# Hybrid encoder layer with hierarchical experts: first gather straight from the slot table, block table between weight splits, token places on GpSimd

## The reference, cut to what matters

```python
# 4 groups x 8 experts, top-1 group, top-2 experts in it: 2048 assignments
n_blocks = -(-n_assign // 128) + 32            # slots in blocks of 128 rows
padded = ((counts + 127) // 128) * 128         # each expert starts a new block
dest = pad_start[e_sorted] + (arange(n_assign) - start[e_sorted])
slot_tok[dest] = tok_sorted;  slot_w[dest] = w_sorted
block_expert = searchsorted(pad_end, block_start, side='right')
x_blocks = h[slot_tok].reshape(n_blocks, 128, 1024)
# each block with its expert's weights, (1024 x 512), (1024 x 512), (512 x 1024):
hid = silu(xb @ w_gate[e]) * (xb @ w_up[e]);  y = hid @ w_down[e]
out = zeros.at[slot_tok].add(y * slot_w)       # and x + out, final RMSNorm
```

## Time and profile before

| | us |
|---|---|
| median of 3 runs (lowest, highest) | 1426.55 (1425.6, 1429.34) |
| the profiled execution | 1429.69 |
| its span, first to last instruction | 1428.0 |
| TensorE busy | 1321.2 (93%) |
| VectorE busy | 1093.4 (77%) |
| ScalarE busy | 861.3 (60%) |
| GpSimd busy | 413.8 (29%) |
| mean granted TensorE clock | 0.973 |

### The profile page before, as it was taken

How to read it: one execution, slowest core, us unless ns; L and a number is a source line. 1 busy time by engine, 2 the same in 40 slices (tenths; PEclk the granted TensorE clock), 3 DMA queues, 4 the chain that set the end, 5 groups by cost and what they waited for, 6 DMA issues and landing times. The chain is left out here.

```text
span 1428.0 us, 25159 instructions
## 1 busy us (share of the span) xinstructions
PE 1321.2 (93%) x8518; PEld 1115.0 (78%) x8518; DVE 1093.4 (77%) x1510; ACT 861.3 (60%) x1162; POOL 413.8 (29%) x473
## 2 busy tenths in 40 slices
PE   4999999978898879999998899999999999999984
PEld 4999778867887878668887788888888888888851
DVE  5895697775778758545667888888888888888837
ACT  7473345565566464552214777777777777777722
POOL 6020089008666737312101111111111111111140
PEclk9999999988999989999998999999999999999997
DMA  9174988412234139811016999999999999999773
GB/s 269 48 227 146 271 249 238 113 41 51 47 94 128 26 118 337 317 43 78 31 45 232 363 404 418 407 415 409 409 414 409 411 410 414 407 410 412 317 280 157
DMA packets 154825, 357.51 MB, mean 250 GB/s; under 512 B 43999, under 2 KB 100603, under 8 KB 127483
## 3 DMA queue, kind: packets, MB, share of 16 engines
q1 hardware_dynamic: 131899, 297.04, 55.8%
q0 software_dynamic: 14976, 40.43, 8.3%
q10 hardware_dynamic: 7872, 19.01, 3.4%
HBM read 287.64 MB, written 68.78 MB: 250 GB/s over the span
## 5 line engine op out<-in xcount | busy, mean ns | idle before, releaser
L2908 PE MATMUL gate_up_mm<-w_hi,gathered_T_hi 128*128 128x512 f32 x528 | 212.3, 402 | 7.7 <-DVE gathered_T_lo L3103 7.7
L2910 PE MATMUL gate_up_mm<-w_hi,gathered_T_lo 128*128 128x512 f32 x528 | 208.0, 394 | 0.0
L2909 PE MATMUL gate_up_mm<-w_lo,gathered_T_hi 128*128 128x512 f32 x528 | 207.7, 393 | 0.0
L3098 DVE TENSOR_TENSOR w_lo<-w_down,w_hi 128x2048 fp32r<-128x2048 f32 x66 | 148.5, 2289 | 54.0 <-ACT w_hi L3019 54.0
L2842 POOL COPY gather_idx<-upto_pair 128x1 int32 (+1 forms) x34 | 13.1, 385 | 510.8 <-PE x_turned L2898 470.9
L3098 DVE TENSOR_TENSOR w_lo<-first_w_gate,w_hi 128x2048 fp32r<-128x2048 f32 x66 | 150.7, 2289 | 9.5 <-ACT w_hi L3019 8.0
L3019 ACT ACTIVATE w_hi<-w_up 128x2048 fp32r<-128x2048 f32 x66 | 126.6, 1919 | 50.6 <-PE down_mm L2945 50.1
L3098 DVE TENSOR_TENSOR w_lo<-w_up,w_hi 128x2048 fp32r<-128x2048 f32 x66 | 150.6, 2287 | 4.0
L3019 ACT ACTIVATE w_hi<-w_down 128x2048 fp32r<-128x2048 f32 x66 | 125.0, 1918 | 41.2 <-issue 20.8
L3019 ACT ACTIVATE w_hi<-first_w_gate 128x2048 fp32r<-128x2048 f32 x66 | 127.0, 1925 | 32.4 <-PE gate_up_mm L2910 31.6
L2908 PEld LDWEIGHTS gate_up_mm<-w_hi,gathered_T_hi 128*128 128x128 f32 x528 | 100.4, 190 | 34.0 <-issue 12.8
(11 more groups left out here) (522 smaller groups left out, 3100.9 us busy)
## 6 DMA issues: line engine op xcount, KB each, us to landing
w_up<-in_expert_w_up SPq DMA_DIRECT2D x66, 1024.0 KB, 8.5
w_down<-in_expert_w_down SPq DMA_DIRECT2D x66, 1024.0 KB
first_w_gate<-in_expert_w_gate SPq DMA_DIRECT2D x64, 1024.0 KB, 7.6
expert_rows_dram<-ones SPq DMA_DIRECT2D x32, 512.0 KB, 6.8
expert_rows_dram<-expert_out ACTq DMA_DIRECT2D x32, 512.0 KB, 8.5
x<-s_rows_dram SPq DMA_DIRECT2D x9, 1184.0 KB, 6.9
s_rows<-s_rows_dram SPq DMA_DIRECT2D x7, 1184.0 KB, 7.5
w_raw<-in_w_in SPq DMA_DIRECT2D x12, 512.0 KB, 5.2
```

What stands on the lines that cost most here:

```text
L2908: pe.matmul(dst, xT_hi[:, k, :], hi[:, at, cols], start=k == 0, stop=False)
L2909: pe.matmul(dst, xT_hi[:, k, :], lo[:, at, cols], start=False, stop=False)
L2910: mm = pe.matmul(dst, xT_lo[:, k, :], hi[:, at, cols], start=False, stop=k == KT - 1)
L3098: dve.tensor_tensor(lo[:, at, :], flat(j), hi[:, at, :].bitcast(F32), ALU.subtract).then_inc(S["piece_lo"], 1)
```

## The change

- GpSimd's first gather takes its index straight from column 0 of the slot table, with no copy and no wait.
- `block_table` is cut in pieces, `table_starts`, `table_ends` and `table_blocks`. On TensorE the small matmuls of the second half stand behind the turning of block 0's rows; on VectorE the first split of block 0 stands ahead of `table_ends`.
- `rows_rest(0)` stands ahead of the splits 1 to 3 of block 0, `rows_out(1)` and `rows_rest(1)` stand one split earlier.
- `places` leaves VectorE. The gates stay there (`gates`, five operations). The rest is done by GpSimd in its loop, behind its two gathers: `found_places` in i = 1, `final_places` in i = 2, `turned_places` (the picks) in i = 3. The wide comparison becomes 16 operations with a scalar from a column, the reduction over 32 experts five additions by halves, and what was one operation with two steps of which one is a tensor becomes two.
- ScalarE's two exponentials stand behind the four splits of block 0.
- `keep_clock` counts are 5, 10, 16 and a new 16 behind the turning of block 1, where 12, 8 and 8 stood.

```diff
 # GpSimd
-            gather(0, 0, 1)
+            step = Steps(pool, S["small"])
+            def found_places():
+                pool.wait_ge(S["starts"], 1)
+                step(pool.tensor_scalar(E, kept["down_e"][:], -1.0, float(NEXP), ALU.mult, ALU.add))
+                step(pool.tensor_scalar(INV, kept["level"][:], 1.0, None, ALU.min))
+                step.done()
+                for n in range(2 * TT):
+                    step(pool.tensor_scalar(one_e[:, n], iota[:, 0:NEXP], small_cols[:, 0, n:n + 1], None, ALU.is_equal))
+                step.done()
+                step(TTo(one_e[:], one_e[:], starts[:, 0].rearrange("p (o e) -> p o e", o=1).broadcast_to(wide), ALU.mult))
+                step.done()
+                n = NEXP // 2
+                while n > 1:
+                    step(TTo(one_e[:, :, 0:n], one_e[:, :, 0:n], one_e[:, :, n:2 * n], ALU.add))
+                    step.done()
+                    n //= 2
+                step(TTo(small_cols[:, 1], one_e[:, :, 0], one_e[:, :, 1], ALU.add))
+            def final_places():
+                step.done()
+                step(TTo(OV, OV, kept["level"][:], ALU.add))
+                step(pool.tensor_scalar(base[:, 1:2], reach[:, TABLE - 1:TABLE], float(P), float(P), ALU.mult, ALU.subtract))
+                step.done()
...
+                step(pool.tensor_scalar(dest_f[:], place[:], -1.0, base[:, 1:2], ALU.min, ALU.add))
+                step.done()
+                pool.wait_ge(S["gate"], 5)
+                step(TTo(gate_f[:], gate_f[:], rt["gate"][:], ALU.mult))
+                step(pool.tensor_copy(dest[:], dest_f[:]))
+                step.done()
+                pool.sem_inc(S["placed"], 1)
+            def turned_places():
+                for t in range(TT):
+                    for k in range(2):
+                        pool.tensor_scalar(picks[:, t, k, :], iota[:], place[:, k, t:t + 1], rt["gate"][:, k, t:t + 1],
+                                           ALU.is_equal, ALU.mult).then_inc(S["picks"], 1)
+            pool.indirect_dma_start(out=xg[:, 0, :], out_offset=None, in_=h_dram,
+                                    in_offset=bass.IndirectOffsetOnAxis(ap=rt["slot_tok"][:, 0:1], axis=0)
+                                    ).then_inc(gathered[0], 16)
             pool.wait_ge(S["tables"], 3)
...
-                        gather(1 - s, column, b + 2)
+                        gather(1 - s, column, b + 1)
+                with pool.If(i == 1):
+                    found_places()
+                with pool.If(i == 2):
+                    final_places()
+                with pool.If(i == 3):
+                    turned_places()
 # TensorE
-            keep_clock(12)
-            block_table()
-            keep_clock(8)
+            keep_clock(5)
+            table_starts()
+            keep_clock(10)
             pe.wait_ge(gathered[0], 16)
             turn_rows(0)
-            keep_clock(8)
+            table_blocks()
+            keep_clock(16)
             pe.wait_ge(S["xT_lo"], 1)
...
             turn_rows(1)
+            keep_clock(16)
             pe.wait_ge(S["tables"], 3)
 # ScalarE
-            act.activation(kept["group"][:], kept["group"][:], ACT.Exp).then_inc(S["gates"], 1)
-            act.wait_ge(S["small"], 1)
-            act.activation(kept["top"][:, 1], kept["top"][:, 1], ACT.Exp).then_inc(S["gates"], 1)
             for j in range(2):
                 split(0, j, 16, None)
             rows_out(0)
             for j in (2, 3):
                 split(0, j, 16, None)
+            act.activation(kept["group"][:], kept["group"][:], ACT.Exp).then_inc(S["gates"], 1)
+            act.wait_ge(S["top"], 1)
+            act.activation(kept["top"][:, 1], kept["top"][:, 1], ACT.Exp).then_inc(S["gates"], 1)
             silu(2)
...
             split(1, 0, 32, 3)
+            rows_out(1)
             split(1, 1, 32, 4)
-            rows_out(1)
 # VectorE
-            block_table()
-            for j in range(2):
+            table_starts()
+            rest(0, 0, 1)
+            table_ends()
+            table_blocks()
+            rows_rest(0)
+            for j in range(1, 4):
                 rest(0, j, j + 1)
-            rows_rest(0)
-            for j in (2, 3):
-                rest(0, j, j + 1)
-            places()
+            gates()
...
             rest(1, 0, 7)
+            rows_rest(1)
             rest(1, 1, 8)
             hidden(0, 4)
-            rows_rest(1)
```

More of the change, by code:

```diff
@@ L2733, in experts @@
              "y_out idx turn small picks picked_mm picked last sum par add sq ms rt rs res "
-             "reach reach_turned past tables block_step gates placed").split()
+             "reach reach_turned past tables block_step gates top starts gate placed").split()
     S = {n: core.sem("ex_" + n) for n in names}
@@ L2847, in gather, with of @@
                                         ).then_inc(gathered[s], 16)
-            gather(0, 0, 1)
+            step = Steps(pool, S["small"])
+            TTo = pool.tensor_tensor
+            def of(n):
+                return small_cols[:, n].rearrange("p (k t) -> p k t", k=2)
+            E, OV, INV = (of(n) for n in range(3))
+            wide = [P, 2 * TT, NEXP]
+            def found_places():
[14 more added lines that the diff above has]
+                step(TTo(small_cols[:, 1], one_e[:, :, 0], one_e[:, :, 1], ALU.add))
@@ new lines, in final_places @@
+            def final_places():
[3 more added lines that the diff above has]
+                step.done()
+                step(pool.tensor_scalar(OV, OV, 1.0, None, ALU.subtract))
+                step.done()
+                step(TTo(OV, OV, E, ALU.subtract))
+                step.done()
+                step(TTo(OV, OV, INV, ALU.mult))
+                step.done()
+                step(TTo(OV, OV, E, ALU.add))
+                step.done()
+                step(pool.tensor_scalar(OV, OV, float(P), None, ALU.mult))
+                step.done()
+                step(TTo(dest_f[:], OV, kept["slot"][:], ALU.add))
+                step.done()
+                step(pool.tensor_scalar(place[:], dest_f[:], base[:, 1:2], None, ALU.subtract))
+                step.done()
+                step(pool.tensor_scalar(gate_f[:], place[:], 0.0, None, ALU.is_lt))
+                step(pool.tensor_scalar(dest_f[:], place[:], -1.0, base[:, 1:2], ALU.min, ALU.add))
+                step.done()
+                pool.wait_ge(S["gate"], 5)
+                step(TTo(gate_f[:], gate_f[:], rt["gate"][:], ALU.mult))
+                step(pool.tensor_copy(dest[:], dest_f[:]))
+                step.done()
+                pool.sem_inc(S["placed"], 1)
@@ L2850, in _ @@
+            pool.sem_inc(S["turn"], 1)
             pool.wait_ge(S["tables"], 3)
@@ L2881, in keep_clock, with table_starts @@
                     pe.matmul(y_ps[:, 0, 0:P], c["ident"][:], c["ident"][:], start=True, stop=True)
-            def block_table():
+            def table_starts():
                 pe.wait_ge(S["reach"], 2)
@@ L2888, in block_table, with table_blocks @@
                 pe.transpose(r_ps[0:NEXP, 2 * P:3 * P], starts[:, 1], c["ident"][:]).then_inc(S["reach_turned"], 1)
+            def table_blocks():
                 pe.wait_ge(S["past"], 3)
@@ L3092, in _ @@
         def _(dve):
-            small = Steps(dve, S["small"])
+            gate_step = Steps(dve, S["gate"])
             def rest(s, j, n):
@@ L3110, in hidden, with table_starts @@
                 dve.tensor_tensor(hid[:], sg[:], u_ps, ALU.mult).then_inc(S["hid"], 1)
-            def block_table():
-                step = Steps(dve, S["block_step"])
+            step = Steps(dve, S["block_step"])
+            def table_starts():
                 TTo = dve.tensor_tensor
@@ L3119, in last @@
                     return x.rearrange("p (e o) -> p e o", o=1).broadcast_to([P, x.shape[1], n])
-                small(TTo(kept["top"][:, 1], kept["top"][:, 1], kept["top"][:, 0], ALU.subtract))
                 step(dve.tensor_scalar(reach[:, 0:NEXP], iota[:, 0:NEXP], 1.0, None, ALU.add))
@@ L3134, in block_table, with table_ends @@
                 step.done()
-                step(TTo(starts[:, 0], starts[:, 1], starts[:, 0], ALU.subtract))
+                TTo(starts[:, 0], starts[:, 1], starts[:, 0], ALU.subtract).then_inc(S["starts"], 1)
+                TTo(kept["top"][:, 1], kept["top"][:, 1], kept["top"][:, 0], ALU.subtract).then_inc(S["top"], 1)
+            def table_ends():
                 dve.wait_ge(S["reach_turned"], 1)
@@ L3143, in block_table, with table_blocks @@
                                       ).then_inc(S["past"], 1)
+            def table_blocks():
+                TTo = dve.tensor_tensor
                 dve.wait_ge(S["reach_turned"], 2)
@@ L3153, in block_table, with gates @@
                 dve.tensor_copy(rt["block"][:], found[:, 1]).then_inc(S["tables"], 1)
[L3155 to L3161, removed]
+            def gates():
                 TTo = dve.tensor_tensor
```

(12 more changed lines are left out.)

## The result

The changed kernel takes 1446.12 us (median of 4 runs, 1443.13 to 1453.14) against 1426.07 for the kernel before (4 runs): ratio 1.0149, 95% interval 1.0127 to 1.0170, slower by 20.05 us. Forecast was 1431.6, range 1419.5 to 1440. The sign was right, the time is outside the range. It equals the second rival's 1446, but by chance: that rival is 1.1 us of gain and 20.7 us of cost over three late gathers, measured are a gain of 8.5 and a cost of 29.4 over two.

A forecast was written before the change was run, and what follows sets the result against it. TensorE, busy every microsecond from 834.1 to 1352 us, was taken as the bound, so its waits add whole. Run-up gain 6.3 against late-gather cost 11.4 (7.0 + 4.4) gives +5.1 on 1426.55: 1431.6 us, range 1419.5 to 1440.

The forecast's parts named there:

- rival 2: Gather 1 late (gain 1.1) and all three GpSimd pieces make the next gather late, 20.7 us cost: 1446; chance 0.12.
- Run-up: From the stage's start to block 1's matmuls: earlier first matmul, full clock, earlier gather 1; gain 6.3 us, 1.1 to 7.5.
- Gather 1: Second gather in the run-up: copy at the seam at 769.3, issue at the 771.6 gap, landed 781; late end 784.3.
- The loop entry: Before block 1's first matmul, after turning and keep_clock(16): estimated 0.4 us, first matmul at 786.4.
- Rival 3: GpSimd fits, but gather 1 is late and keep_clock(16) runs at half clock: gain 1 to 3, about 1424.5; chance 0.13.
- GpSimd's prices: GpSimd's places work in its loop: found_places 5.7 us, final_places 3.3, turned_places 4.2; 0.12 a comparison, 0.26 a pick.
- The room beside the splits: Steady blocks: three pairs of VectorE splits leave GpSimd 4.2 us of each 17.86 us block.
- The cost of a late gather: TensorE waits for rows behind found_places, 7.0 us with clock loss, and behind turned_places, 4.4: 11.4 us in all.
- the alternative of 9.6 + 2.3: Gather behind found_places: if its issue misses the gap, it waits for the w_down pair, costing 9.6 + 2.3.
- What leaves GpSimd free: VectorE operations fed from PSUM leave GpSimd free; if not, 2.1 us a block would be lost and the forecast later.
- final_places: GpSimd's round 2, 13 operations, 3.3 us: fits into the first three gaps and costs nothing; else as turned_places.
- Rival 1: GpSimd's work fits and gathers land in time, leaving only the 6.3 us gain: 1420.3; chance 0.30.

The follow-up runs named there:

- e8: Changed kernel with the VectorE half of each split made a one-input operation, low parts of the weights left out: 16 comparisons 7.5 us, 16 picks 18.6 us.
- e1: Changed kernel with GpSimd's work on the places cut into pieces over rounds 1 to 9 of its loop: 1416.89 us, ratio 0.9945 to the kernel before.
- e2: Changed kernel with each gather of the loop waiting for one turning fewer, places work as it is: 1417.40 us, ratio 0.9948 to the kernel before.

## Why the prediction was right or wrong

- **Run-up, forecast gain 6.3 (1.1 to 7.5): measured 8.5, above both bounds.** Mechanism right. The first weight matmul came 2.25 us earlier (forecast 1.8), the 48 took 11.0 (11.1), at clock 1.00. Gather 1's copy ended at 769.77 with the split of 767.44 (2.28 long) as put; its issue ran in the next gap, begun at 770.59, and block 1 was turned about 1.4 us sooner than I had it. The loop entry, 0.4 in the forecast, cost nothing (the last keep_clock pass ends at 785.08, the next matmul starts at 784.93). Counted as in the forecast the first matmul of block 1 stands at 784.2, not 786.4. Rival 3 and the late gather 1 of rival 2 fell.
- **GpSimd's prices: the step that failed.** I took 0.12 us a comparison from the starts of two IOTAs and 0.26 a pick from VectorE's row. Measured alone: 0.35 and 0.79. `found_places` is then about 9 us (0.5 + 5.3 + 1.3 + 1.95 for the additions by the formula of the earlier trace rows, an estimate), not 5.7, and `turned_places` 12.4, not 4.2. The upper bound of 0.4 an operation held the comparison and not the pick.
- **The room beside the splits: right in kind.** 4.2 us a block was the room I found; 12.4 us of picks took 35.6 us, two blocks with 8.4 us of it. By this count some 4 us were won at seams, at VectorE's cost: its pair of w_up splits went from 4.72 to 5.84 in the block with the product and the additions, which is off the path:

```profile
838.61 5.84 DVE L3175 TENSOR_TENSOR w_lo<-w_up,w_hi 128x2048 fp32r<-128x2048 f32 x2
```

- **The cost of a late gather: 7.0 and 4.4 forecast, 14.9 and 14.5 measured.** This is what the prices and the room made of it. The forecast's times are those of the kernel before; the changed kernel is 7.6 us earlier there (-8.3 and 0.74 for the later start of the stage). In its own times I had the copy behind `found_places` at 844.6, the issue over by 846.4, the rows landed at 855.1 and wanted at 850.2. Measured: copy at 851.21, issue from 852.97 to 855.73, turned from 863.2, 12.7 us of wait. The work had run on into the pair of w_down splits, which is the alternative of 9.6 + 2.3 that I named and did not take; even that is 3 us short, since the issue then met a split of the next pair too and took 2.76 us. For the picks the issue was over at 943.8, 13 us later than forecast (the gather ahead of the picks started 78.85 us later than the one of 824.89, so the forecast's 851.6 is 930.4). The clock's share, 2.1 and 1.8 forecast, was 2.1 and 1.6.
- **What leaves GpSimd free.** The forecast used the time of VectorE's operations fed from PSUM as free for GpSimd and gave as evidence the copy that ended at 769.41. The row below shows how thin that is: the copy ended 0.12 us after `gathered_T_lo` began and 0.04 after the splits. The rows of e8 show it properly.

```profile
769.29 1.22 DVE L3103 TENSOR_TENSOR gathered_T_lo<-x_turned,gathered_T_hi 128x1024 fp32r<-128x1024 f32 x1
```

- **final_places: nothing, as forecast.** It ran in 8.3 us (867.88 to 876.14). Even where no hole helped it, in e1, it took 12.1 us and the next copy still waited for TensorE. Rival 2 had this piece late too, from a price of 0.35 us an operation, which is the price measured for a comparison; it still ended in time.
- **Rival 1** (only the gain is left) has the time of e1 and e2, 1417, with the gain of 8.5 in place of 6.3. They reach it by pieces and by an earlier gather; in the changed kernel itself the work did not fit.

The sum with measured terms: 1426.07 - 8.5 + 14.9 + 14.5 = 1447.0, measured 1446.12. The best version is e1, faster than the kernel before by 0.55% (0.37 to 0.73%) and than the changed one by some 29 us.

## What to carry to other kernels

An engine that issues the loads is on the path as soon as its other work outlasts the slack to its next issue: put work behind a load in pieces shorter than that slack, or issue the load a block earlier; either took the whole loss away here. Price an operation on the engine that will run it, in its form, and then by the gaps that its neighbour leaves; a row from another engine is no price. In a run-up in which several things end at about the same time, the parts don't add up: here one part gave 0.5 us alone and 4.1 as the last, another 3.1 alone and 1.6 as the last.

## What the runs showed of the hardware that was not expected

- A GpSimd `tensor_scalar` of 128x128 with two scalar columns takes 0.79 us (VectorE: 0.26), of 128x32 with one 0.35, with nothing beside it.
- An operation of one input on VectorE, 1.23 us long, keeps GpSimd off as the one with two inputs does: a 0.22 us addition took 1.24. One with an input in PSUM does not: three operations of 0.23 to 0.30 us kept these times beside it.
- Moving 16 such picks off VectorE (4.2 us) gave GpSimd 35.6 us of work, and the steady blocks lost at most 0.2 us in all by it once it was spread.
